# The RWKV scan of a hybrid diffusion block: the transposed inverse is kept with the two heads of a pair exchanged, so that products run interleaved over four 64x64 tiles

## The reference, cut to what matters

```python
def step(S, inp):
    r_t, w_t, k_t, v_t, kk_t, b_t = inp
    sa = -jnp.einsum("bhvk,bhk->bhv", S, kk_t)
    S = S * w_t[:, :, None, :] + sa[..., None] * b_t[:, :, None, :] + v_t[..., None] * k_t[:, :, None, :]
    return S, jnp.einsum("bhvk,bhk->bhv", S, r_t)
S, ys = lax.scan(step, state0, xs, reverse=reverse)
```

## Time and profile before

| what | value |
|---|---|
| median of 3 runs | 2486.52 us (2484.43 to 2492.95) |
| the profiled execution | time 2487.39 us, span 2485.6 us |
| mean granted TensorE clock | 0.938 |
| busy over the span: PE, DVE, ACT, POOL | 2196.0, 1312.9, 927.3, 346.0 us |
| scan of layer 0 | about 265 to 520 us of the span |
| scan of layer 1 | about 1683 to 1930 us of the span |

### The profile page before, as it was taken

One profiled execution on the slowest core, in us unless ns is written; L12 is line 12 of the kernel. 1 busy time (PEld: TensorE's weight loads), 2 busy tenths in 40 slices (PEclk: granted clock), 3 DMA queues, 4 the chain that ended last, 5 costly groups with the idle time before them and its releaser, 6 DMA issues. The chain is left out here.

```text
span 2485.6 us, 47863 instructions
## 1 busy us (share of the span) xinstructions
PE 2196.0 (88%) x19929; PEld 1732.0 (70%) x19929; DVE 1312.9 (53%) x1958; ACT 927.3 (37%) x1605; POOL 346.0 (14%) x445
## 2 busy tenths in 40 slices
PE   6897688879989998889998987968888798998998
PEld 2374688845557887668887833837888566997998
DVE  5756777772372333343332267477777515455544
ACT  4633344422342222232222156334444234444442
POOL 1001533300100011010000011024333020010000
PEclk9999899987999999999999988989999879998999
DMA  8640000030111332222232375400000302453543
GB/s 283 237 144 1 2 0 2 0 113 20 34 37 51 96 100 85 68 85 88 100 102 85 102 235 185 144 1 1 0 2 1 131 1 87 137 177 122 184 164 125
DMA packets 157295, 219.47 MB, mean 88 GB/s; under 512 B 6815, under 2 KB 123769, under 8 KB 156129
## 3 DMA queue, kind: packets, MB, share of 16 engines
q1 hardware_dynamic: 155648, 215.74, 25.7%
q0 software_dynamic: 1504, 1.71, 0.2%
HBM read 208.00 MB, written 9.44 MB: 87 GB/s over the span
## 5 line engine op out<-in xcount | busy, mean ns | idle before, releaser
L332 DVE TENSOR_TENSOR W_low<-RING,W_high 128x1024 fp32r<-128x1024 f32 x364 | 445.0, 1231 | 483.1 <-ACT W_high L329 482.5
L329 ACT ACTIVATE W_high<-RING 128x1024 fp32r<-128x1024 f32 x364 | 380.4, 1053 | 663.0 <-PE BANK L370 628.5
L368 PE MATMUL BANK<-H_high,W_high 128*128 128x512 f32 (+2 forms) x1472 | 526.1, 357 | 77.7 <-ACT H_high L584 35.7
L370 PE MATMUL BANK<-H_high,W_low 128*128 128x512 f32 (+2 forms) x1472 | 519.6, 353 | 0.0
L369 PE MATMUL BANK<-H_low,W_high 128*128 128x512 f32 (+2 forms) x1472 | 519.6, 353 | 0.0
L368 PEld LDWEIGHTS BANK<-H_high,W_high 128*128 128x128 f32 (+1 forms) x1472 | 283.2, 192 | 132.5 <-issue 51.7
L370 PEld LDWEIGHTS BANK<-H_high,W_low 128*128 128x128 f32 (+1 forms) x1472 | 283.5, 193 | 37.9
L369 PEld LDWEIGHTS BANK<-H_low,W_high 128*128 128x128 f32 (+1 forms) x1472 | 284.0, 193 | 36.9 <-issue 1.1
L1169 PE MATMUL BANK<-RING,WORK 64*64 64x64 f32 x4096 | 165.9, 220 | 17.3 <-DVE RING L1122 8.7
L1169 PEld LDWEIGHTS BANK<-RING,WORK 64*64 64x64 f32 x4096 | 144.8, 135 | 29.8 <-issue 29.6
L974 POOL TENSOR_TENSOR WORK<-WORK,masks 128x256 f32<-128x256 f32 x160 | 126.7, 804 | 113.2 <-PE BANK L1169 112.7
(11 more groups left out here) (277 smaller groups left out, 3412.2 us busy)
## 6 DMA issues: line engine op xcount, KB each, us to landing
RING<-w_mod_dram SPq DMA_DIRECT2D x48, 1024.0 KB, 5.0
RING<-w_in_dram SPq DMA_DIRECT2D x46, 1024.0 KB, 5.1
RING<-w_ffn_in_dram SPq DMA_DIRECT2D x44, 1024.0 KB, 5.0
RING<-w_ffn_out_dram SPq DMA_DIRECT2D x22, 1024.0 KB, 4.7
RING<-w_out_dram SPq DMA_DIRECT2D x8, 1024.0 KB, 5.0
h_high<-H_high SPq DMA_DIRECT2D x2, 2048.0 KB, 6.4
h_low<-H_low SPq DMA_DIRECT2D x2, 2048.0 KB, 11.9
H_high<-h_high SPq DMA_DIRECT2D x2, 2048.0 KB, 10.7
```

What stands on the lines that cost most here:

```text
L329: high_ready.mark(nc.scalar.activation(self.part(0, c), self.raw(c), ACT.Copy))
L332: low_ready.mark(nc.vector.tensor_tensor(self.part(1, c), self.raw(c), self.part(0, c).bitcast(FP32), ALU.subtract))
L368: nc.tensor.matmul(out, w[0], x[0], start=start, stop=False)
L370: return nc.tensor.matmul(out, w[1], x[0], start=False, stop=stop)
```

## The change

The transpose of the inverse, T2[:, 1], is now kept with the two heads of a pair exchanged (head 0 on DOWN, head 1 on UP). The products that read or make it go from UP to DOWN and from DOWN to UP (`across`), so that they use the two quarters of the array that their partners leave free, and a new function `both` issues a straight and a crossed product in turn:

- Gram: the width 128 products for B_LT (straight) and for B_G (crossed, so `gram_out` reads the heads exchanged) are interleaved, 32 instructions; the width 64 product for B_L comes last. The wait for the operands of B_G (`s_ops`, `s_y_out`) now stands ahead of all of them.
- Merge in levels 1 to 4: the product for T (straight, now in B_L) and that for its transpose (crossed, in B_LT) are interleaved, 32 instructions. X1 is made crossed, and so are W and SA; their count is as before.
- DVE: T2's start was one instruction, PSUM 128x512 times mask (1108). It is now three: two of 64x256 with both inputs in SBUF (LTS of one half times mask, written to the other half), and one of 128x256 from PSUM. The subtraction (1122) reads two half banks instead of one bank. Nothing else changes in count.

```diff
-        B_L, B_LT, B_G, B_S = 0, 1, 2, 3
+        B_LT, B_L, B_G, B_S = 0, 1, 2, 3
+        ACROSS = ((UP, DOWN), (DOWN, UP))
...
-                        dve.wait_ge(*at_step(s_gram[d], i, 3, 3))
-                        for h, rows in enumerate((UP, DOWN)):
+                        dve.wait_ge(*at_step(s_gram[d], i, 3, 2))
+                        for h, rows in enumerate((DOWN, UP)):
...
-                        both = BANK[:, 4 * d + B_L:4 * d + B_LT + 1].rearrange("p b (j n) -> p b j n", j=PAIRS)[:, :, :, 0:HD]
                         dve.wait_ge(*at_step(s_lts[d], i, 1, 1))
-                        dve.wait_ge(*at_step(s_gram[d], i, 3, 2))
-                        s_first[d].mark(nc.vector.tensor_tensor(T2[d], both, masks[:, d, 0:2].unsqueeze(2).to_broadcast([P, 2, PAIRS, HD]), ALU.mult))
+                        for here_rows, there in ACROSS:
+                            nc.vector.tensor_tensor(T2[d][there, 1], LTS[d][here_rows], masks[here_rows, d, 1].unsqueeze(1).to_broadcast([HD, PAIRS, HD]), ALU.mult)
+                        dve.wait_ge(*at_step(s_gram[d], i, 3, 3))
+                        s_first[d].mark(nc.vector.tensor_tensor(T2[d][:, 0], pairs(4 * d + B_L, 0), lanes(masks[:, d, 0]), ALU.mult))
...
-                                s_t[d].mark(nc.vector.tensor_tensor(T2[d].rearrange("p q j t -> p (q j t)"), T2[d].rearrange("p q j t -> p (q j t)"),
-                                                                    BANK[:, 4 * d + B_LT], ALU.subtract))
+                                s_t[d].mark(nc.vector.tensor_tensor(T2[d].rearrange("p q j t -> p q (j t)"), T2[d].rearrange("p q j t -> p q (j t)"),
+                                                                    BANK[:, 4 * d + B_LT:4 * d + B_L + 1, 0:HALF], ALU.subtract))
...
+                def both(width, straight, crossed):
+
+                    for j in range(PAIRS):
+                        for across, (bank, lhs, rhs) in enumerate((straight, crossed)):
+                            for rows, there in ACROSS:
+                                last = nc.tensor.matmul(BANK[there if across else rows, bank, j * width:(j + 1) * width],
+                                                        lhs(j)[rows], rhs(j)[rows], start=True, stop=True)
+                            if j == PAIRS - 1 and not across:
+                                straight_last = last
+                    return straight_last, last
...
-                        hold(pe)
-                        s_gram[d].mark(each(bank + B_LT, 0, 2 * HD, lambda j: BK[d][:, j, 0], qr))
-                        s_gram[d].mark(each(bank + B_L, 0, HD, q, lambda j: BK[d][:, j, 0], 2 * HD))
                         pe.wait_ge(*at_step(s_ops[d], i, 1, 1))
                         if need_y:
                             pe.wait_ge(*at_step(s_y_out[d], i - y0))
                         hold(pe)
-                        s_gram[d].mark(each(bank + B_G, 0, 2 * HD, lambda j: BK[d][:, j, 1], qr))
+                        for last in both(2 * HD, (bank + B_LT, lambda j: BK[d][:, j, 0], qr), (bank + B_G, lambda j: BK[d][:, j, 1], qr)):
+                            s_gram[d].mark(last)
+                        s_gram[d].mark(each(bank + B_L, 0, HD, q, lambda j: BK[d][:, j, 0]))
...
-                                s_x1[d].mark(each(4 * d + B_L, 0, HD, lambda j: LM[d][:, j], lambda j: T2[d][:, 0, j]))
+                                s_x1[d].mark(each(4 * d + B_L, 0, HD, lambda j: LM[d][:, j], lambda j: T2[d][:, 0, j], across=True))
...
-                                each(4 * d + B_LT, 0, HD, lambda j: T2[d][:, 1, j], lambda j: X1[d][:, j])
-                                s_tx[d].mark(each(4 * d + B_LT, HALF, HD, lambda j: X1[d][:, j], lambda j: T2[d][:, 1, j]))
+                                s_tx[d].mark(both(HD, (4 * d + B_L, lambda j: X1[d][:, j], lambda j: T2[d][:, 1, j]),
+                                                  (4 * d + B_LT, lambda j: T2[d][:, 1, j], lambda j: X1[d][:, j]))[1])
...
-                        s_sa[d].mark(each(4 * d + B_LT, 0, HD, lambda j: T2[d][:, 1, j], lambda j: WS[d][:, j]))
+                        s_sa[d].mark(each(4 * d + B_LT, 0, HD, lambda j: T2[d][:, 1, j], lambda j: WS[d][:, j], across=True))
```

More of the change, by code:

```diff
@@ L1163, in _, with each, halves @@
             def _(pe):
-                def each(bank, at, width, lhs, rhs, stride=None):
-                    stride = stride or width
+                def each(bank, at, width, lhs, rhs, across=False):
                     for j in range(PAIRS):
-                        for rows in (UP, DOWN):
-                            last = nc.tensor.matmul(BANK[rows, bank, at + j * stride:at + j * stride + width],
+                        for rows, there in ACROSS:
+                            last = nc.tensor.matmul(BANK[there if across else rows, bank, at + j * width:at + (j + 1) * width],
                                                     lhs(j)[rows], rhs(j)[rows], start=True, stop=True)
                     return last
+                def both(width, straight, crossed):
+                    for j in range(PAIRS):
+                        for across, (bank, lhs, rhs) in enumerate((straight, crossed)):
+                            for rows, there in ACROSS:
+                                last = nc.tensor.matmul(BANK[there if across else rows, bank, j * width:(j + 1) * width],
[3 more added lines that the diff above has]
+                    return straight_last, last
                 def heads():
                     return [(2 * j + h, j, rows) for j in range(PAIRS) for h, rows in enumerate((UP, DOWN))]
-                def halves(bank, at, out_rows, out_cols, lhs, rhs, k_rows):
+                def halves(bank, at, out_rows, out_cols, lhs, rhs, k_rows, across=0):
                     for j in range(PAIRS):
@@ L1181, in halves @@
                             k = of_head(h, k_rows)
-                            last = nc.tensor.matmul(BANK[of_head(h, out_rows), bank, at + j * HD + out_cols.start:at + j * HD + out_cols.stop],
+                            last = nc.tensor.matmul(BANK[of_head(h ^ across, out_rows), bank, at + j * HD + out_cols.start:at + j * HD + out_cols.stop],
                                                     lhs[k, j, out_rows], rhs[k, j, out_cols], start=True, stop=True)
@@ L1221, in step @@
                             if l < NL:
-                                s_x1[d].mark(each(4 * d + B_L, 0, HD, lambda j: LM[d][:, j], lambda j: T2[d][:, 0, j]))
+                                s_x1[d].mark(each(4 * d + B_L, 0, HD, lambda j: LM[d][:, j], lambda j: T2[d][:, 0, j], across=True))
                             else:
-                                s_x1[d].mark(halves(4 * d + B_L, 0, later_half(d), first_half(d), LM[d], T2[d][:, 0], first_half(d)))
+                                s_x1[d].mark(halves(4 * d + B_L, 0, later_half(d), first_half(d), LM[d], T2[d][:, 0], first_half(d), across=1))
                         for d in range(NDIR):
@@ L1242, in step @@
                         for g, j, rows in heads():
-                            last = nc.tensor.matmul(BANK[rows, 4 * d + B_L, j * HD:(j + 1) * HD], QRG[d][:, g, 0], STATE_V[d][:, g],
+                            there = DOWN if rows is UP else UP
+                            last = nc.tensor.matmul(BANK[there, 4 * d + B_L, j * HD:(j + 1) * HD], QRG[d][:, g, 0], STATE_V[d][:, g],
                                                     start=True, stop=True)
```

## The result

The changed kernel took 2534.08 us (median of 4 runs, 2523.17 to 2538.81), the kernel before 2488.36 (4 runs, 2484.43 to 2492.95): ratio 1.0174, 95% interval 1.0137 to 1.0212. The forecast was 2508, with a range to 2524: the direction was right and the size too small, 46 us where 20 were forecast. The profiled execution took 2532.41 us, 45.0 more than the profiled one of before.

The account below looks back on a forecast made before the run. DVE was taken to bound each step mostly through level 4, then PE and ACT. 2486.5 + 2 for work + 9.5 + 9.5 for clock falls gave 2507.5, say 2508 us; 8-in-10 range 2484 to 2524.

Parts of the forecast that it names:

- The merge: Merges, levels 1 to 4: 0.47 us instead of 0.93; on the path only in level 1, -0.46 us a step.
- The row of level 5: Profile row of 32 loads on 32x32 tiles, 13 ns each, cited against the skill's 25 ns floor.
- The Gram products: Head of each step: interleaving cuts 1.86 us from 4.64, worth nothing on the path because DVE is late.
- DVE: T2's start at the head: three instructions for one, 0.39 us more a direction; +0.75 us a step taken.
- POOL and DVE block each other: Rival: blocking brings DVE to its upper bound, 14 us instead of 2 over the scans; 2520 us, chance 0.10.
- The clock: Sparser PE: falls after level 5 in 13 steps instead of 5, at the head in 12 of 16; +9.5 us each.
- DVE's +2 us: Both scans at one clock: +0.75 for DVE, -0.46 and -0.15 at level 1, +0.14 us a step, sixteen steps.
- the clock's +19 us: Clock falls over sixteen steps: +9.5 us after level 5 and +9.5 us at the head; bounds nothing to +29.
- Clock unchanged: Rival: sparser PE brings no more clock falls, only the +2 us remains; 2489 us, chance 0.17.
- The four tiles do not run at once: Rival: merge and Gram keep their time, DVE's +0.75 us a step stands alone; 2498 us, chance 0.12.
- Faster: Rival: levels 1 to 4 wait for PE, so each gains 0.46 us; -1.1 us a step, 2469 us, chance 0.14.

Follow-up runs that it names:

- Gram alone: The kernel before with only the Gram products interleaved; merges, T2 and DVE's work as before: 2499.64 us, ratio 1.0062.
- PSUM as the source: The changed kernel with DVE's two new small instructions reading the triangle from PSUM instead of LTS in SBUF: 2515.21 us, ratio 1.0114.
- the wide spare products: The changed kernel plus a few unread products, 256 or 512 columns wide, before X1 of direction 0, levels 4 and 5, and level 5's merge: 2503.16 us.
- the row of runs set side by side: Several runs compared by time from last Gram product to X1 of direction 1: from 3.3 us (kernel before, no head falls) to 6.4 (changed kernel, sixteen).
- the best variant: The changed kernel with PE making the transpose's crossed start, and spare products only before level 5 and its merge: 2483.36 us, ratio 0.9984.
- one set after the other: The changed kernel with straight and crossed products of Gram and merges issued as successive sets instead of interleaved: 2527.57 us, ratio 1.0159.
- the short spare products: The changed kernel plus 78 unread instructions a step, at level 1, ahead of levels 3 to 5 and the last merge: 2534.47 us, ratio 1.0203.

## Why the prediction came out too low

**The merge, right.** 14.5 ns from start to start on four 64x64 tiles, 0.46 us gained on the path, as put. The floor of about 25 ns of the Trainium skill ("TensorE: Matmul & The Clock Gate", section "Wait — 56ns, not 53.3ns?") does not hold for these: in the trace four of them start every 58 ns from 484.83 to 485.18. (The row of level 5 that the prediction set against it was one of weight loads, not of products.)

**The Gram products, right in themselves.** Nothing gained on the path; they make the hole in the head, as put. The run with Gram alone shows both.

**DVE, direction right, size off.** Forecast +0.75 on the path, measured 1.40. Three instructions cost 0.85 + 0.42 and two gaps, 1.33 us to the identity's start, where one cost 0.71: +0.62 a direction, not 0.39, for the small SBUF ones take 0.43 here and not the 0.34 from start to start that I took. In direction 1 comes 0.43 from POOL's level-2 mask. In direction 0, 0.36 is given back by the identity (1.67 instead of 2.03), and the state update ends 0.12 later. 0.62 + 0.43 + 0.62 - 0.36 + 0.12 = 1.43, against 1.40 read. So the rival "POOL and DVE block each other" is true beside the forecast, not instead of it; I had kept it apart with 0.10. The Trainium skill, "SBUF — State Buffer", section "Who interferes with whom", says that a DVE instruction with two SBUF inputs contends with a GpSimd instruction that reads SBUF, and that one with at most one SBUF input does not. The trace agrees: 1.28 us for the pair with LTS while POOL is at it, 0.86 with PSUM as the source, 0.85 when POOL comes later.

At full clock a step is then 1.40 - 0.61 = +0.79 by these terms, +0.88 by the clean step of 32.14; forecast was +0.14. Over sixteen steps 14 us instead of 2.

**The clock, place right, size off.** Both places were named. At the head a fall came in 16 of 16 steps, not 12, for 32.94 - 32.14 = 0.8 us where it is late, after the merge of direction 0 has been issued, and more where it begins before X1 of direction 1 and lasts 6.8 us, as in 334.52. In the tail it came in 11 (forecast 13), but for more than the 1.2 us carried over from before: steps that have it last 34.59, 34.90 and 35.64 against 32.94, of which 0.1 to 0.4 is the longer or earlier fall at their head (level 5 starts that much later) and the rest, 1.5 to 2.3, the tail. There the fall begins earlier, or lasts up to 10 us instead of 3.4, and covers more of the chain. For the fourteen steps: 14 x 0.88 = 12 from work at full clock, about 14 x 0.9 = 13 at the head, nine tail falls at about 2 = 18, less some 6 that before had paid: 37, against 36.9 read. The two last steps, with both falls long, add 13.9. This split was made from typical steps after the result was known, so that it meets 36.9 is no proof of its terms.

**The failed step** is therefore the size of two terms, DVE's +2 us (measured 14) and the clock's +19 us (measured some 37 over the sixteen steps, the last ones included). They are coupled, which my bounds did not say: a later X1 is itself what widens the hole ahead of it. I gave the two their upper bounds singly, and the range ended below their sum; and the clock's 37 lie above its own bound of 29 too, which put 1.3 us on a fall in the tail and 0.95 on one at the head, and had none of 6.8 or 10.2 us in it. That the clock carries most is shown by the wide spare products (31 us less with more work; 0.44 us a step of it, some 7 us, is not the clock but POOL's changed place). That a thin head brings the falls there is shown by the Gram products alone, and that a later X1 brings more by the row of runs set side by side; that the lateness alone would do is not shown. In the 37 are also PE's stops without a data wait, at most 6.7 us, which the prediction had no term for; a fall of 10.2 us follows in each step that has them, but there is one such fall without a stop too, and whether a stop brings it was not tested.

**The rivals.** "Clock unchanged" fell: no step without a fall. "The four tiles do not run at once" fell by the 14.5 ns. "Faster" fell as put: the eight subtractions of the step still have only 1.2 us of idle before them, the levels 2 to 4 wait for DVE.

**Still open.** Why PE stands still with "issue" as the only reason, before falls of the clock. The steps are written as two loops a layer, over the four context and the first three latent steps, with the eighth step written out behind them. Of 37 such stops of over 1.5 us within the scans of all traces, 31 lie in the first pass of a loop or in the eighth step, where the code runs for the first time. A longer PE program is not needed: the changed kernel has 19929 PE instructions like the kernel before. That PE waits for its own instructions was not isolated. Partly for this reason the 1.02 us a step of the best variant do not reach the total, and no version here clearly beats the kernel before.

## What to carry to other kernels

Before packing products denser, ask whether PE waits at that place: if it does, the time saved becomes idle, and can cost more through the granted clock than the products ever took. Price such falls together with what makes the next product late, because each enlarges the other. And when work is taken over from PE by DVE to make a layout possible, try the reverse: here 16 more PE instructions a direction were cheaper than two small DVE instructions on the path (clean steps of 30.24 us against 32.14). And when an experiment is to take an effect away, look in its trace whether it is gone: one set after the other still overlapped.

## What was not expected of the hardware

- The clock at the head fell in sixteen of sixteen steps, and stayed down for 3.4 to 6.8 us; in the tail for up to 10.2, where the earlier trace rows show 3.41.
- A few spare products of 256 and 512 columns, with a result nobody reads, took 31 us off a kernel (2534 to 2503); the mean granted clock of the fourteen steps went from 0.87 and 0.89 to 0.99 and 0.98.
- PE can stand still for 2 to 4 us with all its data there (4.06 at 372.56 with the short spare products, 2.27 at 1862.62 in the changed kernel), mostly where code runs for the first time.
- Two sets of 64x64 products for different quarters of the array overlap even when one is issued behind the other: 32 merge instructions start within 0.65 to 0.70 us, against 0.91 on two quarters and 0.48 interleaved.
